# Rounding and subtracting each slot of weights in two halves, issued in neighbouring slots of the mixers' schedules

## The reference

```python
for l in range(2):
    if l == 0: h = even_mixer(x, ...)   # x @ w_in (1024 x 3584); 4 heads of a gated linear recurrence (HGRN2),
                                        # 4 heads of differential attention; concatenated @ w_out
    else:      h = odd_mixer(x, ...)    # x @ w_in (1024 x 4112); 16 heads of forgetting attention (FoX); @ w_out
    x = layer_norm(ALPHA * x + h)
    gate, up = split(x @ w1, 2)         # w1: 1024 x 5632
    x = layer_norm(ALPHA * x + (silu(gate) * up) @ w2)   # w2: 2816 x 1024
```

## Time and profile before

| | us |
|---|---|
| median of 3 runs | 1579.8 (1579.32 to 1583.16) |
| span of the profiled execution | 1576.7 |
| PE busy in it | 1484.2 (94%) |
| ACT, DVE, POOL busy | 529.7, 502.5, 496.3 |

### The profile page before, as it was taken

How to read it: one execution, slowest core, us unless ns; L and a number is a source line. 1 busy time by engine, 2 the same in 40 slices (tenths; PEclk the granted TensorE clock), 3 DMA queues, 4 the chain that set the end, 5 groups by cost and what they waited for, 6 DMA issues and landing times.

```text
span 1576.7 us, 19745 instructions
## 1 busy us (share of the span) xinstructions
PE 1484.2 (94%) x7532; PEld 1233.4 (78%) x7532; DVE 502.5 (32%) x1116; ACT 529.7 (34%) x873; POOL 496.3 (31%) x213
## 2 busy tenths in 40 slices
PE   7999989889999999999979999879899999999997
PEld 6898876467888888877878888777688888888875
DVE  3355443655311111010663444352435111110104
ACT  4523233542323232211244554453513323222120
POOL 4222121103343443534133222211133444444340
PEclk9999999688999999999999999998899999999999
DMA  6211102102233333322122111002021333323211
GB/s 222 81 54 29 52 27 80 54 1 81 60 101 107 95 92 94 111 89 80 56 81 81 54 54 54 27 1 108 27 81 54 107 87 100 107 67 133 79 68 54
DMA packets 136469, 118.07 MB, mean 75 GB/s; under 512 B 5428, under 2 KB 112052, under 8 KB 136376
## 3 DMA queue, kind: packets, MB, share of 16 engines
q1 hardware_dynamic: 136376, 116.82, 24.3%
HBM read 114.71 MB, written 2.10 MB: 74 GB/s over the span
## 4 chain that ended last, share of the span: by engine, by line
PE 83%; DVE 8%; ACT 6%; issue 2%; POOL 0%; DMA 0%; ACTq 0%; POOLq 0%; DVEq 0%; SPq 0%
PE banks L453 23%; PE banks L454 23%; PE banks L455 23%; PE banks L907 2%; PE banks L889 2%; PE banks L723 2%; ACT w_hi L1004 1%; PE banks L524 1%; PE banks L822 1%; PE banks L898 1%; PE banks L742 1%; ACT p_fox L1253 1%; DVE fox_ms L1560 1%; DVE o_even L1430 1%; PE banks L853 1%
## 5 line engine op out<-in xcount | busy, mean ns | idle before, releaser
L964 POOL TENSOR_TENSOR w_lo<-w_raw,w_hi 128x1024 fp32r<-128x1024 f32 (+1 forms) x209 | 496.1, 2394 | 1042.9 <-ACT w_hi L1004 1042.9
L453 PE MATMUL banks<-xT_lo,w_hi 128*128 128x512 f32 (+2 forms) x912 | 344.2, 377 | 3.2 <-DVEq L1307 3.2
L454 PE MATMUL banks<-xT_hi,w_lo 128*128 128x512 f32 (+2 forms) x912 | 341.9, 375 | 0.0
L455 PE MATMUL banks<-xT_hi,w_hi 128*128 128x512 f32 (+2 forms) x912 | 341.7, 375 | 0.0
L1004 ACT ACTIVATE w_hi<-w_raw 128x2048 fp32r<-128x2048 f32 (+1 forms) x107 | 200.0, 1869 | 220.6 <-PE banks L455 184.2
L453 PE MATMUL banks<-w_lo,xT_hi 128*128 128x512 f32 (+1 forms) x608 | 225.4, 371 | 10.0 <-ACT o_fox L1026 3.9
L454 PE MATMUL banks<-w_hi,xT_lo 128*128 128x512 f32 (+1 forms) x608 | 216.4, 356 | 0.0
L455 PE MATMUL banks<-w_hi,xT_hi 128*128 128x512 f32 (+1 forms) x608 | 216.2, 356 | 0.0
L453 PEld LDWEIGHTS banks<-xT_lo,w_hi 128*128 128x128 f32 (+1 forms) x912 | 172.3, 189 | 34.0 <-issue 4.2
L455 PEld LDWEIGHTS banks<-xT_hi,w_hi 128*128 128x128 f32 (+1 forms) x912 | 172.1, 189 | 31.2
L454 PEld LDWEIGHTS banks<-xT_hi,w_lo 128*128 128x128 f32 (+1 forms) x912 | 172.3, 189 | 29.8
(11 more groups left out here) (177 smaller groups left out, 1460.2 us busy)
## 6 DMA issues: line engine op xcount, KB each, us to landing
w_raw<-in_ffn_w_dram SPq DMA_DIRECT2D x92, 512.0 KB, 4.4
w_raw<-in_ffn_w_dram SPq DMA_DIRECT2D x20, 1024.0 KB, 5.0
w_raw<-in_fox_w_in_dram SPq DMA_DIRECT2D x16, 1024.0 KB, 5.6
w_raw<-in_even_w_in_dram SPq DMA_DIRECT2D x14, 1024.0 KB, 5.2
w_raw<-in_even_w_out_dram SPq DMA_DIRECT2D x4, 1024.0 KB, 5.0
w_raw<-in_fox_w_out_dram SPq DMA_DIRECT2D x4, 1024.0 KB, 6.4
x_res<-in_x_dram SPq DMA_DIRECT2D x4, 512.0 KB, 7.8
out_dram<-x_res SPq DMA_DIRECT2D x4, 512.0 KB, 2.6
```

The lines of the kernel that those rows point to most:

```text
L453: mm(acc, l_hi, r_lo, start=first, stop=False)
L454: mm(acc, l_lo, r_hi, start=False, stop=False)
L455: return mm(acc, l_hi, r_hi, start=False, stop=final)
L964: ins = nc.gpsimd.tensor_tensor(w_lo[c % RING][:, a:a + n], w_raw[c % RAW][:, a:a + n], w_hi[c % RING][:, a:a + n].bitcast(F32), ALU.subtract)
```

## The change

Both the rounding and the subtraction of a chunk are cut in two halves of up to 1024 elements, and `hi_ready` and `lo_ready` count halves. POOL may start on the first half when that half is rounded. ACT's calls in the mixers are moved: in the even mixer the first half goes to b = 2 and the second stays at b = 3; in the differential attention the halves go to s = 5 and 7, 9 and 11; in FoX to pieces 1 and 2. Everywhere else `hi_upto` issues both halves in a row. Loads wait as before for the whole chunk to be subtracted.

```diff
             def weights_in(c):
-                pe.wait_ge(hi_ready, c + 1)
-                pe.wait_ge(lo_ready, c + 1)
+                pe.wait_ge(hi_ready, 2 * (c + 1))
+                pe.wait_ge(lo_ready, 2 * (c + 1))
...
                 if c >= RAW:
-                    sp.wait_ge(lo_ready, c - RAW + 1)
+                    sp.wait_ge(lo_ready, 2 * (c - RAW + 1))
...
             for c, (_, _, size) in enumerate(chunks):
-                pool.wait_ge(hi_ready, c + 1)
                 if c >= RING:
                     pool.wait_ge(*chunk_used[c - RING])
-                for a in range(0, size, 1024):
-                    n = min(1024, size - a)
-                    ins = nc.gpsimd.tensor_tensor(w_lo[c % RING][:, a:a + n], w_raw[c % RAW][:, a:a + n],
-                                                  w_hi[c % RING][:, a:a + n].bitcast(F32), ALU.subtract)
-                ins.then_inc(lo_ready, 1)
+                n = size // 2
+                for part in range(2):
+                    a = part * n
+                    pool.wait_ge(hi_ready, 2 * c + part + 1)
+                    nc.gpsimd.tensor_tensor(w_lo[c % RING][:, a:a + n], w_raw[c % RAW][:, a:a + n],
+                                            w_hi[c % RING][:, a:a + n].bitcast(F32), ALU.subtract
+                                            ).then_inc(lo_ready, 1)
...
             def hi_upto(n):
-                while rounded[0] < min(n, len(chunks)):
-                    c = rounded[0]
-                    act.wait_ge(w_loaded[c % RAW], need[c])
-                    if c >= RING:
-                        act.wait_ge(*chunk_used[c - RING])
-                    size = chunks[c][2]
-                    chain(fn(w_hi[c % RING][:, 0:size], w_raw[c % RAW][:, 0:size], ACT.Copy), hi_ready)
+                hi_halves(2 * n)
+
+            def hi_halves(n):
+
+                while rounded[0] < min(n, 2 * len(chunks)):
+                    c, part = rounded[0] // 2, rounded[0] % 2
+                    if part == 0:
+                        act.wait_ge(w_loaded[c % RAW], need[c])
+                        if c >= RING:
+                            act.wait_ge(*chunk_used[c - RING])
+                    m = chunks[c][2] // 2
+                    a = part * m
+                    chain(fn(w_hi[c % RING][:, a:a + m], w_raw[c % RAW][:, a:a + m], ACT.Copy), hi_ready)
                     rounded[0] += 1
...
-                hi_upto(a + 2 if b < 2 else a + 3) if b == 1 or b == 3 else None
+                if b >= 1:
+                    hi_halves(2 * (a + 2) + (b - 1) % 3)
...
-                if s in (1, 5, 9):
-                    hi_upto(stage_chunks["a_g"][0] + 2 + s // 4)
+                if s in (1, 3, 5, 7, 9, 11):
+                    hi_halves(2 * (stage_chunks["a_g"][0] + 1 + s // 4) + 1 + s // 2 % 2)
...
-                if piece and piece[1] == 1:
-                    hi_upto(piece[0] + 3)
+                if piece and piece[1] in (1, 2):
+                    hi_halves(2 * (piece[0] + 2) + piece[1])
```

## The result

The changed kernel is slower: median 1588.28 us of 10 runs (1582.72 to 1590.28) against 1575.93 of 10 (1572.91 to 1583.16), a ratio of 1.0068 with a 95% interval of 1.0054 to 1.0082, or some 10.7 us (the two medians lie 12.4 us apart). The forecast was 1587, or +7.0 over the profiled execution; its span is 1587.2 against 1576.7.

The account below looks back on a forecast made before the run. PE, busy 94% of the span, bounds the kernel. Terms 0.25 + 0.3 - 1.7 + 9.1 - 1.0 = +7.0 us on 1576.7 give 1583.7 of span, plus 3.1 around it 1587; range 1571 to 1595.

Parts of the forecast that it names:

- Sign and mechanism: Slower by more than 0.3%, chance 0.54; likeliest case, chance 0.5: POOL's earlier start stalls DVE in the even mixer.
- FoX: FoX: six q and k chunks 0, between -5 and +3; two roundings in a row at 809, -1.0 us.
- The slot at 168 to 176: Even mixer: two POOL stalls ahead of `k_dec` where one was, +4.1 us; PE's wait near 6.5 us.
- The slots at 122 and 200: Even mixer: exponential delayed, POOL stalls DVE's multiplications; PE's product 2.1 to 4.4 and 2.0 to 4.2 late, net +2.2 us each.
- Even mixer in sum: Even mixer: 2.2 + 4.1 + 2.2 + 0.6 = +9.1 us, between -6 and +12.
- the clock: New PE waits of 2 to 4 us in four slots could bring two slow-clock stretches: 1594 us, chance 0.12.
- the wait moves by one slot, 0: FoX q and k slots: PE's wait of 1.64 us nearly goes but reappears a slot later, 0 for six chunks.
- The waits for weights: Two PE waits for `w_lo`: `lo_ready` comes 0.86 us earlier, 1.4 becomes some 0.5 each, -1.7 us.
- The price of a split: ACT: halves of 1.06 us, 2.16 in place of 1.92 per chunk; +0.25 at the start, +0.3 in norms.
- DVE's held instructions: DVE's instructions stalled by POOL: their number stays the same in the profile after.
- Rival (b): Nothing: POOL's stalls of DVE change place and not number; 1579 to 1581 us, chance 0.18.
- Rival (a): Relief: halves fall into hand-over gaps, waits for `k_dec`, `qA` and weights shrink; -11 us, or 1569, chance 0.2.

Follow-up runs that it names:

- e1: The changed kernel with the even mixer alone put back, both halves in a row at b = 3; ratio 0.9973 to the kernel before.
- e3: The changed kernel with even mixer, differential attention and FoX put back, so halves issued in a row; ratio 0.9958 to the kernel before, 1571.33 us.
- e12: The kernel before, chunks whole, with the even mixer's rounding at b = 2 in place of b = 3; ratio 1.0111 to the kernel before.

## Why the prediction was right, and where its terms were not

*Sign and mechanism* held: the likeliest case and not a rival, POOL's earlier start in front of DVE. *The size* is in part luck. +7.0 was forecast, and +10.5 of span and 0.68% were measured, but of the sum's terms the even mixer was 10.3 us too low (+9.1 against 19.4), while 9.9 us came back later where -1.0 for FoX and -1.7 for the weights had been put. The 3.1 us added to the span were too much as well: in the changed kernel's runs the time is 1.8 above the span. And the kernel before, whose median of 1579.8 (three runs) stands behind the 1587, has 1575.93 in ten.

*The slot at 168 to 176* came out as worked: POOL on the first two instructions of the norm, `k_dec` unheld, a wait near 6.5 forecast and 6.46 measured.

*The slots at 122 and 200*: PE's product was put at 2.1 to 4.4 us late; it waits 3.57 and 0.43 in front of it, so the worse order held, narrowly. DVE's second multiplication was issued 0.16 us after POOL's second half. What I gave back for it was too much. I let PE's later wait of 1.71 and DVE's lateness absorb 1.1; in the trace PE still waits 1.32 at line 747, because DVE's chain begins behind PE's own late product.

*Even mixer in sum*: +9.1 forecast. In the matched traces it is 19.4 between 25 and 260 us. In the times the place alone is 0.95% or 15 us (e1), and e1 itself has the loss of the halves in this stage that e3 showed. The term that was mis-sized is the clock, which I left out of the sum as a rival. In the even mixer there are now four stretches of 6.8 us at half clock, where there was one of 3.4 and one of 6.8: 17 us more at half, worth 8.5. Apart from the clock 10.9 are left, against 9.1. Of these 1.2 are a place that I did not see, near 64 us, where line 453 waits 1.0 us for `qT`. It is the same meeting once more:

```profile
52.20 5.06 POOL L964 TENSOR_TENSOR w_lo<-w_raw,w_hi 128x1024 fp32r<-128x1024 f32 x2 [13.72 <-ACT w_hi L1004]
52.51 2.50 DVE L1358 TENSOR_SCALAR kT<-kT 128x512 f32<-128x512 f32 x1
```

```profile
52.39 4.93 POOL L965 TENSOR_TENSOR w_lo<-w_raw,w_hi 128x1024 fp32r<-128x1024 f32 x2 [13.71 <-ACT w_hi L1011]
52.57 2.50 DVE L1364 TENSOR_SCALAR q_dec<-kT 128x512 f32<-128x512 f32 x1
55.11 2.50 DVE L1365 TENSOR_SCALAR k_dec<-kT 128x512 f32<-128x512 f32 x1
```

Before (the first two lines) POOL held one of DVE's instructions; after, it starts earlier against them and holds two, so the chain to `qT` is later.

*FoX* was put at -1.0. It gives back 5.4 in the matched traces, 4.4 apart from the clock. The step that failed is "the wait moves by one slot, 0": it let the 0.86 us by which the first slot's chain is earlier be used up in the next one. In the traces POOL's earlier start alone (halves in a row, nothing moved) is worth some 6 us in FoX, and the second place takes back only 1.2. Near 950 us there are two smaller waits in place of one:

```profile
961.69 1.55 DVE L1568 TENSOR_SCALAR fox_ms<-fox_ms 128x4 f32<-128x4 f32 x1
...
966.09 0.60 PE L853 MATMUL banks<-ident,qn 128*66 128x128 f32 x4 [0.83 <-ACT qA L1282]
...
968.10 1.50 DVE L1568 TENSOR_SCALAR fox_ms<-fox_ms 128x4 f32<-128x4 f32 x1
...
972.34 0.60 PE L853 MATMUL banks<-ident,qn 128*66 128x128 f32 x4 [1.06 <-ACT qA L1282]
```

0.83 and 1.06 add up to more than the 1.64 of the earlier trace rows, so here the wait did move by a slot, as forecast. But neither is followed by a half clock, as the one was, and that saves 3.1 us at this place (12.9 behind at 953, 9.8 at 961). Over the whole stage the time at half clock fell only from 25.9 to 23.9 us, so most of it was paid elsewhere. At 809 the gain was 1.8 (3.45 and 0.44 in place of 4.21 and 1.53), not 1.0.

*The waits for weights* came out at 0.6 each, -1.6 in all, as forecast. *The price of a split*: two halves start 1.09 us apart at 1.06 each, as the trace of before had said; a chunk's rounding in two takes 2.16 us in place of 1.92. The Trainium skill (ScalarE: Activation LUTs, What ACT_TABLE_LOAD costs) gives an overlap of about 93 ns between activations back to back. It is not seen between these halves, of which each waits for the one before it.

*DVE's held instructions* were to keep their number. Counting those that take over 0.3 us longer than the shortest of their line and shape, masked merges left out, there are 35 before and 32 after. In FoX the small one of lines 1560 and 1568 is held 8 times before and 12 after.

*Rival (b)*, that the stalls only change place, has the right premise: POOL's busy time is nearly the same (498.7 against 496.3 us). The Trainium skill (SBUF — State Buffer, SBUF: two separate sides) calls the port pair of DVE and GpSimd an exclusive lock, held for the whole instruction. The rows shown here agree with it: instructions of 0.17 and 0.43 us take 2.02 to 2.45 beside a subtraction of 2.35. The rule says how long a stall is, but not whether it lies in front of what PE waits for; e12 and e1 show that this decides some 1%. *Rival (a)* was right in sign for the halves without the places (e3, -0.42%), by FoX and the weights; the waits for `k_dec`, from which it took half of its gain, grew there from 10.0 to 13.0.

## What to carry to other kernels

When a background task of another engine shares a port with a link of the critical chain, look for what it meets when it starts, not for how long it is: here a start 0.8 us earlier cost 3 us of wait at one place, and earlier starts gave some 6 in another stage. Split such a task if you like, but keep each part behind the exponential or root that DVE is already waiting for. Measure the split and each new place apart: one change here held a gain of 0.4%, a loss of 0.9% and a smaller loss of 0.2 to 0.5%. Where the clock comes and goes with short waits, compare the parts of a trace with its share taken off.

## What the runs showed of the hardware

A DVE instruction of 128x4 elements, 0.17 us alone, takes 2.06 and 2.27 us when it meets a running subtraction on POOL; one of 128x256, 0.43 alone, takes 2.02 and 2.45. The size of the held instruction hardly matters. Of two POOL instructions in a row each holds one of DVE's in these rows, and one of DVE's gets in between them. Not held are merges from PSUM with a mask (COPY_PREDICATED: 0.74 us at 172.79 in the kernel before, with a subtraction running, and 0.74 at 168.75 with none) and DVE's sums (line 1567: the 12 that began under a subtraction in the changed kernel took 0.42 us each, as the others did). Waits of 3.57 us on PE were followed by some 6.8 us at half clock, those of 0.83 and 1.06 near 970 by none.
